# Modulation's sums as transposes, attention's copies in another order on four banks, and the front in two halves of the features

## The reference

```python
cond_lat, cond_ctx = silu(c), silu(c_ctx)           # two condition vectors of 1024
m = cond @ w_mod[layer] + b_mod[layer]              # 6 x 1024 values for each: shift, scale, gate, ...
u = h * (1 + m[1]) + m[0]                           # x (512 tokens) by cond_lat, ctx (256 tokens) by cond_ctx
q, k, v, p = split(u @ w_mix_in)                    # k and v for all 768 tokens, q and p for the 512
o = softmax(q k^T / 8) v                            # 8 heads in 2 groups of kv, 512 x 768 scores each
pool = window means of p, by a 128x128 matrix for each of 4 groups
y = concat(o, pool) @ w_mix_out
```

## Time and profile before

| what | us |
|---|---|
| median of 3 runs | 3259.61 (3253.62 to 3261.14) |
| the profiled execution, own time | 3256.57 |
| its span, first to last instruction | 3254.8 |
| PE busy in it | 2835.5 (87%) |
| DVE / ACT / POOL busy | 1123.0 / 746.1 / 130.7 |
| mean granted TensorE clock | 0.928 of full |

### The profile page before, as it was taken

The page is one execution under the profiler, slowest core; times in us unless marked ns, Lnnn a source line. Parts: engine busy times, 40 slices in busy tenths (PEclk is TensorE's granted clock), DMA queues, the critical chain, the costliest instruction groups (busy, mean ns, idle before and its releaser), DMA issues.

```text
span 3254.8 us, 31937 instructions
## 1 busy us (share of the span) xinstructions
PE 2835.5 (87%) x13512; PEld 1830.4 (56%) x13512; DVE 1123.0 (35%) x1546; ACT 746.1 (23%) x1114; POOL 130.7 (4%) x120
## 2 busy tenths in 40 slices
PE   6977879888849979988885997999979999989997
PEld 4634444323328644423334764888769865468886
DVE  4344331111153351211125533333331488233233
ACT  2233210100021130100013412222221265132121
POOL 1210200000010020000001000000010000000000
PEclk8988989999969979999997998999987899989998
DMA  7852169999932138999991212232240300113321
GB/s 275 294 197 56 34 276 428 427 428 428 427 135 78 66 129 339 428 428 428 426 391 57 78 52 71 85 107 74 98 127 3 78 1 1 38 67 102 105 85 39
DMA packets 122254, 600.99 MB, mean 185 GB/s; under 512 B 7184, under 2 KB 12560, under 8 KB 96256
## 3 DMA queue, kind: packets, MB, share of 16 engines
q1 hardware_dynamic: 117056, 584.27, 45.5%
q0 software_dynamic: 5056, 14.69, 1.5%
HBM read 596.84 MB, written 2.10 MB: 184 GB/s over the span
## 4 chain that ended last, share of the span: by engine, by line
PE 67%; DMA 15%; DVE 11%; ACT 5%; issue 1%; POOL 0%; DVEq 0%; ACTq 0%; POOLq 0%
PE psum L281 65%; ACT scratch L269 5%; DMA weight_ring<-in_w_exp_down 5%; DVE scratch L231 4%; DMA weight_ring<-in_w_exp_up 4%; DMA scratch<-in_w_exp_down 3%; DMA weight_ring<-in_w_exp_gate 3%; PE psum L296 2%; DVE scratch L3020 1%; DVE scratch L244 1%; DVE scratch L264 1%; DVE scratch L1288 1%; DVE scratch L237 1%; DMA weight_ring<-in_w_mod 1%; DVE scratch L239 1%
## 5 line engine op out<-in xcount | busy, mean ns | idle before, releaser
L281 PE MATMUL psum<-scratch,scratch 128*128 128x512 f32 (+14 forms) x9424 | 1924.0, 410 | 133.3 <-DVE scratch L231 64.1
L281 PEld LDWEIGHTS psum<-scratch,scratch 128*128 128x128 f32 (+4 forms) x9424 | 1406.2, 188 | 641.3 <-issue 295.2
L281 PE MATMUL psum<-weight_ring,scratch 128*64 128x512 f32 (+2 forms) x2752 | 714.3, 622 | 105.0 <-ACT scratch L269 35.6
L281 PEld LDWEIGHTS psum<-weight_ring,scratch 128*64 128x64 f32 (+2 forms) x2752 | 241.9, 146 | 527.2 <-issue 398.6
L231 DVE TENSOR_TENSOR scratch<-weight_ring,scratch 128x2048 fp32r<-128x2048 f32 (+2 forms) x110 | 241.9, 2199 | 552.2 <-ACT scratch L269 550.8
L269 ACT ACTIVATE scratch<-psum 128x512 f32<-128x512 f32 (+4 forms) x324 | 188.1, 580 | 820.3 <-PE psum L281 509.1
L269 ACT ACTIVATE scratch<-weight_ring 128x2048 fp32r<-128x2048 f32 (+2 forms) x110 | 202.9, 1844 | 614.2 <-PE psum L281 582.3
L296 PE MATMUL psum<-consts,scratch 128*128 128x128 f32 (+1 forms) x984 | 158.0, 306 | 126.6 <-DVE scratch L237 60.8
L231 DVE TENSOR_TENSOR scratch<-scratch,psum 128x512 f32<-128x512 f32 x92 | 63.3, 688 | 561.2 <-PE psum L281 559.7
L231 DVE TENSOR_TENSOR scratch<-scratch,scratch 128x512 fp32r<-128x512 f32 (+10 forms) x334 | 207.6, 622 | 80.0 <-ACT scratch L269 69.7
L296 PEld LDWEIGHTS psum<-consts,scratch 128*128 128x128 f32 (+1 forms) x984 | 124.9, 164 | 177.1 <-issue 97.0
(11 more groups left out here) (100 smaller groups left out, 606.7 us busy)
## 6 DMA issues: line engine op xcount, KB each, us to landing
weight_ring<-in_w_exp_gate SPq DMA_DIRECT2D x40, 2048.0 KB, 18.8
weight_ring<-in_w_exp_up SPq DMA_DIRECT2D x38, 2048.0 KB, 20.6
weight_ring<-in_w_exp_down SPq DMA_DIRECT2D x38, 2048.0 KB, 20.7
weight_ring<-in_ffn_w SPq DMA_DIRECT2D x28, 2048.0 KB, 7.8
scratch<-in_w_exp_up SPq DMA_DIRECT2D x26, 2048.0 KB, 20.6
scratch<-in_w_exp_down SPq DMA_DIRECT2D x26, 2048.0 KB, 18.1
weight_ring<-in_w_mod SPq DMA_DIRECT2D x24, 2048.0 KB, 8.7
scratch<-in_w_exp_gate SPq DMA_DIRECT2D x24, 2048.0 KB, 20.6
```

The lines of the kernel that those rows point to most:

```text
L281: ins = T.eng.matmul(out, lhsT, rhs, start=start, stop=stop)
```

## The change

1. **Sums.** `sum_cols` and its load are gone. `sums` now makes four full transposes of the parts, and `sum_out` has two DVE instructions: a reduction over the four partial sums, read from the transposed bank (32 elements of each partition), and the addition of the bias. This holds for all 24 halves.
2. **Front.** The first four halves are loaded as halves 0 and 2, then the k and v weights, then halves 1 and 3. Halves 0 and 2 are shift and scale of features 0 to 511. The products, sums, modulation and the k and v matmuls are made for these features first, and then for the others. x and ctx are loaded in two parts of 512 features; the second part and all that POOL issues behind it wait for half 2. The products and sums use banks 4, 5 and 6, 7.
3. **Attention.** The ring `TURNED` has four banks (4 to 7), and the values use it too. ACT's copy of the first transposed bank of step n-2 stands ahead of the exponentials of step n, the copy of the values one step earlier, right behind the exponentials. DVE's copy stands ahead of `normalise`.

The first three hunks, left out below, take away `sum_cols`: its constant, its two columns in `consts`, and its load in `Start.pool`.

```diff
@@ -545,12 +540,12 @@
-    def products(self, T, j):
+    def products(self, T, j, ring=None):
         k, m = self.k, self.m
         T.wait_ge(*k.at("landed", (*self.key, j)))
         T.wait_ge(*k.at("cond", 1))
         w = k.ring.pieces[(*self.key, j)]
-        bank = k.psum.take(T, (*self.key, j), self.ring)
+        bank = k.psum.take(T, (*self.key, j), ring or self.ring)
         for r in range(2):
             for g in range(4):
                 c = 4 * r + g
@@ -568,7 +563,7 @@
             s = slice(n, HALF, 4) if 6 <= i < 10 else slice(n * P, (n + 1) * P)
-            mm(T, bank[:, 2 * n:2 * n + 2], self.part(i)[:, s], k.sum_cols, True, True, *names)
+            tr(T, k, bank[:, n * P:(n + 1) * P], self.part(i)[:, s], *names)
@@ -587,10 +582,10 @@
         V.wait_ge(*k.at("full", *self.key, "sum", i))
-        bank = k.psum.of((*self.key, "sum", i))
-        tt(V, self.m["cols"][:, 4 * i:4 * i + 4, :], bank[:, 0:8].rearrange("p (a b) -> p a b", b=2),
-           self.m["bias_cols"][:, 4 * i:4 * i + 4].unsqueeze(2).to_broadcast([P, 4, 2]), ALU.add,
-           ("free", *self.key, "sum", i))
+        bank = k.psum.of((*self.key, "sum", i)).rearrange("p (n g r) -> p n r g", n=4, g=4)
+        cols = self.m["cols"][:, 4 * i:4 * i + 4, :]
+        reduce(V, cols, bank[:, :, 0:2, :], ALU.add, ("free", *self.key, "sum", i))
+        tt(V, cols, cols, self.m["bias_cols"][:, 4 * i:4 * i + 4].unsqueeze(2).to_broadcast([P, 4, 2]), ALU.add)
@@ -620,43 +615,23 @@
     FIRST = 4
-    ORDER = (0, 2, 1, 3)
-    BANKS, SUMS = (4, 8), (0, 4)
+    BANKS, SUMS = (4, 6), (6, 8)
...
-    def load_rows(self, Y, r):
-        self.k.ring.load(Y, (*self.key, "rows", r), rows(self.k.dram["w_mod"][self.layer], 2 * r, 2 * r + 2, 0, 2 * D))
...
-    def pe(self, T):
-        k, m = self.k, self.m
-        T.wait_ge(*k.at("cond", 1))
-        for r in range(4):
-            piece = (*self.key, "rows", r)
-            T.wait_ge(*k.at("landed", piece))
-            w = k.ring.pieces[piece]
-            for j in range(self.FIRST):
-                job = (*self.key, j)
-                bank = k.psum.of(job) if r else k.psum.take(T, job, self.BANKS)
-                for n in range(2):
-                    g = (2 * r + n) % 4
-                    names = [("full", *job)] if r == 3 and n else []
-                    if j == self.FIRST - 1 and n:
-                        names.append(("weights used", piece))
-                    mm(T, bank[32 * g:32 * g + 32, :], m["cond"][:, 2 * r + n, :], w[:, n, j * HALF:(j + 1) * HALF], r < 2, r >= 2, *names)
-        for j in self.ORDER:
+    def pair_pe(self, T, i):
...
+        for j in (i, i + 2):
+            self.products(T, j, self.BANKS)
+        for j in (i, i + 2):
             self.sums(T, j, self.SUMS)
-    def act(self, A):
-        for j in (0, 1):
-            self.part_out(A, j)
...
-    def dve(self, V):
-        self.bias_dve(V)
-        for j in (2, 3):
-            self.part_out(V, j)
-        for j in self.ORDER:
+    def pair_dve(self, V, i):
+        if i == 0:
+            self.bias_dve(V)
+        self.part_out(V, i + 2)
+        for j in (i, i + 2):
             self.sum_out(V, j)
@@ -913,11 +888,11 @@
         f = self.first
-        for r in (0, 1):
-            f.load_rows(Y, r)
+        for j in (0, 2):
+            f.load_half(Y, j)
         self.kv_units.load(Y)
-        for r in (2, 3):
-            f.load_rows(Y, r)
+        for j in (1, 3):
+            f.load_half(Y, j)
         self.q_units.load(Y)
         for j in (4, 5):
             f.load_half(Y, j)
@@ -928,8 +903,12 @@
         self.first.pool(G)
-        k.loads(G, "xT", [(m["catT"], d["xT"].rearrange("(c p) s -> p c s", p=P)),
-                          (m["raw_ctx"], d["ctxT"].rearrange("(c p) s -> p c s", p=P))])
+        for i in range(2):
+            if i:
+                G.wait_ge(*k.at("landed", ("mod", 0, 2)))
+            n = slice(i * HALF, (i + 1) * HALF)
+            k.loads(G, ("xT", i), [(m["catT"][:, 4 * i:4 * i + 4, :], d["xT"][n].rearrange("(c p) s -> p c s", p=P)),
+                                   (m["raw_ctx"][:, 4 * i:4 * i + 4, :], d["ctxT"][n].rearrange("(c p) s -> p c s", p=P))])
         k.loads(G, "ax", [(self.cos, d["ax_cos"]), (self.sin, d["ax_sin"]),
                           (self.gq, d["q_norm_g"].partition_broadcast(P)), (self.gk, d["k_norm_g"].partition_broadcast(P))])
         G.wait_ge(*G.last())
@@ -941,8 +920,8 @@
-    def inputs(self):
-        for c in range(NC):
+    def inputs(self, half):
+        for c in range(4 * half, 4 * half + 4):
             for i, (x, parts) in enumerate(((self.m["catT"], self.uT), (self.m["raw_ctx"], self.ucT))):
                 yield c, i, x[:, c, :], parts[0][:, c, :], parts[1][:, c, :]
@@ -952,9 +931,11 @@
         k, f = self.k, self.first
-        f.pe(T)
+        f.pair_pe(T, 0)
         run = k.psum.take(T, ("kv", "in"), self.KV, 3).rearrange("p b (t n) -> p (b t) n", t=2)
         for i in range(2):
+            if i:
+                f.pair_pe(T, 1)
             hi, lo = self.kv_units.ready(T, i)
             for c in range(4 * i, 4 * i + 4):
                 T.wait_ge(*k.at("u", c, 0))
@@ -1002,10 +983,11 @@
             self.kv_units.hi(A, i)
-        f.act(A)
-        for c, i, x, hi, lo in self.inputs():
-            A.wait_ge(*k.at("modulated", c, i))
-            act(A, hi, x, ACT.Copy, ("u hi", c, i))
+        for half in range(2):
+            f.part_out(A, half)
+            for c, i, x, hi, lo in self.inputs(half):
+                A.wait_ge(*k.at("modulated", c, i))
+                act(A, hi, x, ACT.Copy, ("u hi", c, i))
         for i in range(2):
             self.q_units.hi(A, i)
@@ -1056,15 +1038,16 @@
             self.kv_units.lo(V, i)
-        f.dve(V)
-        V.wait_ge(*k.at("loaded", "xT"))
-        before = None
-        for c, i, x, hi, lo in self.inputs():
-            ts(V, x, x, cols[:, 8 + c, i:i + 1], cols[:, c, i:i + 1], ALU.mult, ALU.add, ("modulated", c, i))
-            if before:
-                self.input_lo(V, *before)
-            before = c, i, x, hi, lo
-        self.input_lo(V, *before)
+        for half in range(2):
+            f.pair_dve(V, half)
+            V.wait_ge(*k.at("loaded", ("xT", half)))
+            before = None
+            for c, i, x, hi, lo in self.inputs(half):
+                ts(V, x, x, cols[:, 8 + c, i:i + 1], cols[:, c, i:i + 1], ALU.mult, ALU.add, ("modulated", c, i))
+                if before:
+                    self.input_lo(V, *before)
+                before = c, i, x, hi, lo
+            self.input_lo(V, *before)
         for i in range(2):
             self.q_units.lo(V, i)
@@ -1129,7 +1112,7 @@
     KEY = "attention"
-    SCORES, TURNED, VALUES = (0, 4), (4, 7), (7, 8)
+    SCORES, TURNED = (0, 4), (4, 8)
     BUFS = 3
@@ -1243,7 +1226,7 @@
             T.wait_ge(*k.at("free", "pt", *job))
-        bank = k.psum.take(T, ("values", g), self.VALUES)
+        bank = k.psum.take(T, ("values", g), self.TURNED)
         for kt in range(self.NK):
             for i in range(2):
                 mm(T, bank[64 * i:64 * i + 64, :], self.x.v[:, kt, 64 * i:64 * i + 64], self.PT[:, i, kt, :],
@@ -1253,7 +1236,9 @@
         last = len(self.steps)
-        for n in range(last + 4):
+        for n in range(last + 3):
+            if 2 <= n < last + 2:
+                self.turned(A, n - 2, 0, 0)
             if n < last:
                 b = n % self.BUFS
                 A.wait_ge(*k.at("max", n))
@@ -1263,18 +1248,17 @@
                         bias=self.neg[:, b, i:i + 1], scale=1.0, accum_out=self.sum[:, b, i:i + 1])
+            if self.last_of_group(n - 3):
+                g = self.steps[n - 3][0]
+                A.wait_ge(*k.at("full", "values", g))
+                act(A, self.m["catT"][:, g, :], k.psum.of(("values", g)), ACT.Copy, ("free", "values", g))
             if (g := self.pool_step(n - 1)) is not None:
                 A.wait_ge(*k.at("full", "p out", g))
                 act(A, self.m["catT"][:, 4 + g, :], k.psum.of(("p out", g)), ACT.Copy, ("free", "p out", g),
                     scale=self.p_scale[:, g:g + 1])
             if 2 <= n < last + 2:
-                self.turned(A, n - 2, 0, 0)
                 self.turned(A, n - 2, 1, 0)
             self.filler.step_act(A, n)
-            if self.last_of_group(n - 4):
-                g = self.steps[n - 4][0]
-                A.wait_ge(*k.at("full", "values", g))
-                act(A, self.m["catT"][:, g, :], k.psum.of(("values", g)), ACT.Copy, ("free", "values", g))
         A.end(self.KEY)
@@ -1287,10 +1271,10 @@
                     *V.mark(("max", n)))
+            if n >= 2:
+                self.turned(V, n - 2, 0, 4)
             if 1 <= n <= last:
                 self.normalise(V, n - 1)
-            if n >= 2:
-                self.turned(V, n - 2, 0, 4)
             self.filler.step_dve(V, n)
         V.end(self.KEY)
```

(9 more changed lines are left out.)

## The result

| | before | after |
|---|---|---|
| median of 4 runs, us | 3259.56 (3253.62 to 3261.14) | 3213.44 (3212.74 to 3217.38) |
| ratio, 95% interval | | 0.9864 (0.9847 to 0.9881) |
| the profiled execution, its span | 3256.57, 3254.8 | 3217.38, 3215.6 |
| PE busy | 2835.5 | 2805.2 |

The kernel is 46 us faster by these medians and 44 by the ratio; 3214 was predicted. On another chip, with three more rounds, the ratio was 0.9864 again (0.9848 to 0.9879), and the medians differ by 42. The profiled execution after is the slowest of its four, so its trace shows less: the first DVE instruction behind attention comes at 285.10 instead of 326.81, 41.7 us earlier, and what follows is 2.5 us longer than before. In the other twelve traces of this study that last stretch lies between 2922.7 and 2931.4 us without any change in its code, so it is not the change's.

The account below looks back on a forecast made before the run. Bounds: weight loads early in the front, mostly PE from q to attention, then rounds of waits between engines. Terms won 45.8 us: 3256.57 became 3210.8, plus 3.0 for the median, 3214 us; range 3196 to 3238.

Parts of the forecast that it names:

- front, to q's start: Loads, products, sums and modulation before q: q starts at 62.5 us instead of 69.46, 7.0 us won.
- q to attention's first maximum: PE-bound stretch from q to attention: sums as transposes cost 0.53 us plain, 0.97 strided; 5.0 us won.
- steps 0 to 5: Attention's first steps: the product no longer waits for the exponentials; steps 2 to 5 take 5.8 us each; 22.3 won.
- steps 6 to 11: Attention steps where, in all but step 8, the product waits for ACT's values or pooled copy; 67.9 us, 7.0 won.
- steps 12 to 14: Attention's last steps at 5.6, 6.4 and, with values, 10.6 us against 28.7 before; 6.1 us won.
- end: Behind attention's last step DVE's copy, waiting for transposes, stands before the last normalise; 1.6 us lost.
- the far bound of 4.4 us: Front: largest gain for the landing of the k and v weights, 1.57 MB less before them; 3.0 was taken.
- three bounds lie together: Attention's filler steps: next scores at 5.6 us after the exponentials, PE's work 5.5 and DVE near 5.2.
- The bank that is no bound: Rival, attention steps 6 to 11: copies come in time, clock stays up, three steps at 6.6 us; 3202 us, chance 0.18.
- The first terms failing in part: Rival, front and sums: k and v land as before, strided transposes gain nothing; 3225 us, chance 0.13.
- The slow clock through attention: Rival: PE stays at the slow clock in attention, its work per step twice 5.5 us; 3241 us, chance 0.13.
- The slower case: Rival, attention: product stays bound to the exponentials, copy put ahead makes three values steps wait; 3267 us, chance 0.06.

Follow-up runs that it names:

- the last experiment: The changed kernel itself timed and profiled once more beside before, nothing changed, as measure for the other kernels: 3213.74 us, 0.9864.

## Why the prediction was right

The time was right (3214 against 3213.44), and the places of the waits were. That the two agree within a microsecond is luck: in the trace the terms add up to 41.7 and not 45.8, the 3.0 us that were added for the median belong to one execution of before, and the profiled execution after lies 3.9 above its own median. On the marks of the trace:

| term | predicted | in the traces |
|---|---|---|
| front, to q's start | 7.0 | 6.7 |
| q to attention's first maximum | 5.0 | 5.6 |
| steps 0 to 5 | 22.3 | 21.7 |
| steps 6 to 11 | 7.0 | 6.5 |
| steps 12 to 14 | 6.1 | 5.9 |
| end | -1.6 | -4.8 |
| sum | 45.8 | 41.7 (42.5 in the second profile) |

- **Front.** The weights landed at 22.6, not 24.5: 4.9 earlier than before, beyond the far bound of 4.4 us. PE gave it back: the 72 matmuls took 11.57 us instead of 9.6, which I had left as a risk of 1.5. The start of the second half, 49.6, was forecast as 49.2. So two errors of 2 us cancel in this term. It also didn't say whose the 7 us were: 1.5 to 2.7 came from the sums.
- **Sums.** A strided sum costs 0.75, not 0.97, and a plain one 0.66, not 0.53. I had carried the strided weight load's 0.243 over from the two-column form; four transposes with stride take 0.09 more than four without. The Trainium skill's 275 ns for a transpose ("TensorE: Matmul & The Clock Gate", Part 4) is not at odds with that: the four at 101.18 are recorded with a median length of 273 ns each. But they overlap, and the four together take 0.66. Taking four times that figure for a sum, as the prediction did when it put the rule against itself, mixes the length of one with the distance from one to the next. On the marks this stretch won 5.6, with 1.6 lost to the slow clock at 92 us; between the same marks the kernel with the sums alone wins 7.3, so the 5.0 was too small.
- **Steps 0 to 5.** P doesn't wait, ACT's copy is hidden, and three bounds lie together: a filler step is 5.5, 5.6 had been worked out. Undoing attention's part shows 18.1 of the 21.7 to be its own. Unsaid was that in steps 2 and 3 DVE becomes the bound, by POOL's stretch of small additions; I had 5.8 for them, they are 5.9 and 6.3. Steps 0 and 1 are off both ways, 8.3 and 5.5 instead of 7.0 and 7.1: DVE waits 5.96 us (until 143.35) for the load of layer 1's bias, for which 0.2 had been put down, and the slow matmuls fall into step 0.
- **Steps 6 to 11.** The product waits for ACT in steps 6, 7, 9, 10 and 11, and in no other, 2.64 us with the values and 3.25 behind the pooled matmul. Right as written from the order of takes, and shown by taking these waits away. The lengths are 15.9, 11.5, 6.3, 8.8, 14.4 and 11.5 against 14.8, 10.6, 6.6, 10.6, 15.1 and 10.2. The single lengths hang on where the clock happened to fall (step 9 is 8.8 here and 10.4 in the two traces named in the last experiment), so that they add up to 6.5 is in part luck.
- **Whose the 7.0 were, the term doesn't say, and the parts overlap.** Steps 6 to 14 are 103.6 before and 91.2 after. With the new sums and the old order and banks they are 94.3, with the old sums and the new order and banks 95.5 (97.6 with the front changed too). So beside the old order the sums win 9.3 of the 12.4, beside the new one 4.3 to 6.4. In all of attention it is 14.1 or 6.3, where their own rows give 8: the old ones stood on the round of waits, and the clock fell behind them.
- **End.** The term that failed, in its size: -4.8, not -1.6. The wait was named (DVE's copy ahead of the last normalise), its second price was not: PE idle for 3.25 and 1.99 us turns 24 blocks and makes the last values at the slow clock, 2.04 of it in the values alone. Putting the copy back gave 6.0.
- **Rivals.** The bank that is no bound: false as a forecast, but it is what the two moved copies make, 3183. Its premise, that the clock falls only behind idle time, doesn't hold for the old sums (see below). The first terms failing in part: false, the front and the sums gave 12.3 to the first maximum, 12.0 had been put down. The slow clock through attention: false, from 144.5 to 182 us, where PE hardly waits, the granted clock is 1.00. The slower case: false, either edit alone frees the product.

## What to carry to other kernels

Write out the order in which a shared ring's banks are taken and released before giving it another user: here two copies that free a bank and stand behind long instructions made five waits of 2.6 to 3.3 us, and moving them won 28 us, about half of it in work that had run slowly behind the waits. Undo and add each part of a change by itself: the fourth bank without the new order was no worse than both. Ask of each instruction on a round of waits what its neighbours lose, not what its own row says: the new sums won 14.1 us in the old attention and 6.3 in the new, where their rows give 8. Where a late instruction of one engine leaves PE idle (here 2.0 to 3.3 us), look at the lengths of PE's next instructions, too, and in more than one profile.

## What was not expected of the hardware

- PE fell to 0.50 of its clock in the middle of work, behind the old sums of two columns. In the first 345 us of the three traces with these sums (before, the sums undone, attention alone) the recorded clock falls eleven times when PE's last wait of over 0.6 us has ended at least 5 us ago, each time with such sums in between. In the eleven traces with the sums as transposes every fall comes during such a wait or within 1.5 us of its end.
- PE's clock rose while it did nothing but transposes: in the trace with DVE's last steps changed it is 0.50 from 260.5 us on and 1.00 from 264.0, within the 24 transposes at 260.94.
- In the front after, 16 matmuls of 256 columns took 3 us from 33 us on, and 62 took the next 8, at a recorded clock of 1.00 throughout:

```profile
33.00:36.00 3.00, 3.00 (x16) 3.00 (x15) 2.68 (x6) 1.28 (x3) 0.00 (x0) 1.00 1.05 398
36.00:44.00 8.00, 8.00 (x62) 7.87 (x60) 2.47 (x5) 1.05 (x2) 0.00 (x0) 1.00 0.92 335
```

  188 and 129 ns each. The second profile of the same kernel has the same counts in both windows, and its recorded clock is 0.50 until 37.9 us. The first has no record of the clock before 38.7 us, so its 1.00 there says nothing; the lengths do.
- An addition of eight numbers a partition on DVE, from SBUF, took 0.64 to 0.87 us beside POOL's long additions and 0.17 without them; with one input in PSUM it took 0.17 beside them too.
